# A state space computed in blocks of four tokens with a Toeplitz part on TensorE, in a two-layer fp32 decoder trunk

## The reference

```
for l in range(2):
    h = rmsnorm(x, norm_mix[l])
    u, sq, sk, sv, dq, dk, dv, gate_logits = split(h @ w_in[l])
    y_ssm = gelu(s5_ssm(u, ...))                # 32 groups of 16 channels, 64 complex states each
    glu_a, glu_b = split(y_ssm @ ssm_w_glu[l]); y_ssm = glu_a * sigmoid(glu_b)
    y_sb = stick_breaking_attention(sq, sk, sv)
    y_da = rmsnorm(differential_attention(rope(dq), rope(dk), dv, lam)) * (1 - lam_init)
    x = x + sum(sigmoid(gates) * (branches @ w_branch[l])) @ w_out[l]
    m = rmsnorm(mem, norm_mem[l])               # 256 memory tokens, the same in both layers
    x = x + cross_attention(rmsnorm(x, norm_cross[l]) @ w_xq[l], m @ w_xkv[l]) @ w_xo[l]
    x = x + square(relu(rmsnorm(x, norm_mlp[l]) @ w_up[l])) @ w_down[l]
return rmsnorm(x, norm_final)

# s5_ssm, for each group: lam_bar = exp(lam * dt), b_bar = ((lam_bar - 1) / lam) * b
#   s[t] = lam_bar * s[t-1] + b_bar @ u[t];   y[t] = Re(c @ s[t]) + d * u[t]
```

## Time and profile before

| | us |
|---|---|
| median of three runs | 1209.06 (1208.31 to 1209.67) |
| the profiled execution, its own time | 1207.81 |
| its span | 1206.1 |
| TensorE busy in the span | 1090.8 (90%) |
| VectorE busy | 876.0 (73%) |
| ScalarE busy | 565.9 (47%) |
| GpSimd busy | 302.8 (25%) |

### The profile page before, as it was taken

How to read it: one execution, slowest core, us unless ns; L and a number is a source line. 1 busy time by engine, 2 the same in 40 slices (tenths; PEclk the granted TensorE clock), 3 DMA queues, 4 the chain that set the end, 5 groups by cost and what they waited for, 6 DMA issues and landing times. The chain is left out here.

```text
span 1206.1 us, 18306 instructions
## 1 busy us (share of the span) xinstructions
PE 1090.8 (90%) x6855; PEld 963.5 (80%) x6855; DVE 876.0 (73%) x1236; ACT 565.9 (47%) x874; POOL 302.8 (25%) x362
## 2 busy tenths in 40 slices
PE   3997898879999799999979798988899987999996
PEld 3985677769989688998869566767699976998995
DVE  5769999986877475555567899999778756555553
ACT  4643433236565454444444443332475654544442
POOL 0496775510000000000008868653100000000000
PEclk7997988889999989999979988987899998999998
DMA  7652323323554445565646422422255543555550
GB/s 254 184 156 68 109 71 105 100 76 132 184 182 145 128 136 185 187 191 192 186 117 180 122 70 71 124 86 78 98 175 181 177 131 99 183 191 190 184 186 35
DMA packets 138076, 170.34 MB, mean 141 GB/s; under 512 B 18043, under 2 KB 96005, under 8 KB 137989
## 3 DMA queue, kind: packets, MB, share of 16 engines
q1 hardware_dynamic: 137572, 168.91, 44.3%
q10 hardware_dynamic: 416, 0.26, 0.1%
HBM read 168.11 MB, written 1.05 MB: 140 GB/s over the span
## 5 line engine op out<-in xcount | busy, mean ns | idle before, releaser
L1124 DVE TENSOR_TENSOR s_w_lo<-s_raw,s_w_hi 128x1024 fp32r<-128x1024 f32 x312 | 419.5, 1369 | 165.5 <-ACT s_w_hi L742 161.0
L742 ACT ACTIVATE s_w_hi<-s_raw 128x1024 fp32r<-128x1024 f32 x312 | 320.9, 1054 | 186.7 <-PE p_T L1586 114.6
L1584 PE MATMUL p_T<-s_hT_hi,s_w_hi 128*128 128x256 f32 x1152 | 341.9, 297 | 14.2 <-DVE s_hT_lo L1184 14.2
L1585 PE MATMUL p_T<-s_hT_lo,s_w_hi 128*128 128x256 f32 x1152 | 336.8, 292 | 0.0
L1586 PE MATMUL p_T<-s_hT_hi,s_w_lo 128*128 128x256 f32 x1152 | 336.4, 292 | 0.0
L1584 PEld LDWEIGHTS p_T<-s_hT_hi,s_w_hi 128*128 128x128 f32 x1152 | 233.0, 202 | 26.5 <-issue 26.0
L1585 PEld LDWEIGHTS p_T<-s_hT_lo,s_w_hi 128*128 128x128 f32 x1152 | 233.2, 202 | 0.5
L1586 PEld LDWEIGHTS p_T<-s_hT_hi,s_w_lo 128*128 128x128 f32 x1152 | 232.1, 201 | 0.0
L1584 PE MATMUL p_A<-s_w_hi,s_bT_hi 128*128 128x512 f32 x320 | 124.9, 390 | 2.4 <-DVE s_bT_lo L1124 2.4
L1585 PE MATMUL p_A<-s_w_lo,s_bT_hi 128*128 128x512 f32 x320 | 124.7, 390 | 0.0
L1586 PE MATMUL p_A<-s_w_hi,s_bT_lo 128*128 128x512 f32 x320 | 124.5, 389 | 0.0
(11 more groups left out here) (249 smaller groups left out, 1824.4 us busy)
## 6 DMA issues: line engine op xcount, KB each, us to landing
s_raw<-in_w_in SPq DMA_DIRECT2D x104, 512.0 KB, 3.6
s_raw<-in_w_up SPq DMA_DIRECT2D x64, 512.0 KB, 3.7
s_raw<-in_w_down SPq DMA_DIRECT2D x64, 512.0 KB, 3.6
s_raw<-in_w_branch SPq DMA_DIRECT2D x24, 512.0 KB, 3.6
s_raw<-in_w_out SPq DMA_DIRECT2D x16, 512.0 KB, 3.6
s_raw<-in_w_xkv SPq DMA_DIRECT2D x16, 512.0 KB, 3.5
s_raw<-in_ssm_w_glu SPq DMA_DIRECT2D x8, 512.0 KB, 3.5
s_raw<-in_w_xq SPq DMA_DIRECT2D x8, 512.0 KB, 3.5
```

The costliest lines, as they stand in the source:

```text
L742: return nc.scalar.activation(o, i, f, **kw)
L1124: return V.tensor_tensor(o, i0, i1, op)
L1584: mm(o, lhi, rhi, start=first, stop=False, **kw)
L1585: mm(o, lhi, rlo, start=False, stop=False, **kw)
```

## The change

The state space works on blocks of BL = 4 tokens, NB = 64 blocks. State is carried from block to block only: `ssm_in(kb)` (4 of them, 4 tiles each) multiplies u, laid out by blocks in `uB`, by tables `bt` that hold four powers of the decay; VectorE turns, scans 64 blocks with decay to the fourth, and turns back. What happens inside a block is a 4x4 block-Toeplitz matrix `kt` per tile on TensorE, added with `ct` in `ssm_out(kb)`.

These tables (`ct`, `kt`, `bt`, the phase table, the decay `dect`) must be made per layer. Stages `p_spread`, `p_params`, `p_angle`, `p_cos`, `p_ct`, `p_cv`, `p_b0`, `p_bv`, `p_k`, `p_bt` do it on all engines, and `tables` and `zero_b` on POOL. For layer 0 they lie behind units 0 to 6, for layer 1 behind units 50 to 70 of layer 0 (its MLP). The new state space then runs behind units 7 to 12 in layer 0 and 2 to 7 in layer 1. The evacuation of u becomes 32 small copies into `uB` (16 on VectorE, 16 on ScalarE). The memory tokens are read anew in each layer into `att` and transposed behind units 33 and 34; their row statistics are made once, in layer 0, and scale xk and xv. `raw` has 6 slots and `w_hi` 4, so AHEAD falls to 2. The parameters of layer 1 are loaded in layer 0's MLP, ahead of chunk 97 on SP's queue.

```diff
-SSM_STEPS = STILES // 2
+BL = 4
+NB = T // BL
+TAB_STEPS = 6
...
-LO, HI = 10, 6
+LO, HI = 6, 4
 AHEAD = HI // 2
...
+    def pre(tgt, u):
+
+        after(u["angle"], "p_angle", tgt)
+        after(u["cos"], "p_cos", tgt)
+        after(u["ct"], "p_ct", tgt)
+        for r in range(2):
+            after(u["cv"][r], "p_cv", tgt, r)
+        after(u["b0"], "p_b0", tgt)
+        for r in range(2):
+            after(u["bv"][r], "p_bv", tgt, r)
+        for n in range(4):
+            after(u["k"][n // 2], "p_k", tgt, n)
+        for n in range(8):
+            after(u["bt"][n // 2], "p_bt", tgt, n)
+
+    if l == 0:
+        pre(0, dict(angle=0, cos=0, ct=1, cv=(1, 2), b0=3, bv=(3, 4), k=(4, 4), bt=(4, 5, 5, 6)))
+        first = 7
+        pre(1, dict(angle=up0 + 6, cos=up0 + 7, ct=up0 + 9, cv=(up0 + 11, up0 + 13), b0=up0 + 15,
+                    bv=(up0 + 16, up0 + 18), k=(up0 + 18, up0 + 20),
+                    bt=(up0 + 21, up0 + 22, up0 + 23, up0 + 24)))
+        after(up0 + 4, "p_spread", 1)
+        after(up0 + 5, "p_params", 1)
+        for u in (up0 + 4, up0 + 5):
+            side[u].sort(key=lambda s: s[0] != "p_spread")
+    else:
+        first = 2
+    for kb in range(4):
+        after(first + kb, "ssm_in", kb)
+        after(first + 1 + kb, "ssm_out", kb)
+    after(first + 5, "gelu")
...
-    for i in range(SSM_STEPS):
-        after(7 + 2 * i, "ssm_in", i)
-        after(8 + 2 * i, "ssm_rot", i)
-        after(min(10 + 2 * i, 23), "ssm_out", i)
-    after(23, "gelu")
...
-    after(33, "memg")
+    after(33, "mem_turn", 0)
+    after(33, "mem_turn", 1)
+    after(34, "mem_turn", 2)
+    after(34, "mem_turn", 3)
+    if l == 0:
+        after(33, "stats", "mem", 0)
+        after(33, "stats", "mem", 1)
+        after(35, "norm", "mem")
...
+                    if c == 1 and l == 0:
+                        load_params(0)
+                    if c == 2 * AT_UNIT["up", 1, 0] and l + 1 < DEPTH:
+                        sp.wait_ge(*st.at(prm_read, 1))
+                        sp.wait_ge(*st.at(h_ready, 3 * KD // 2))
+                        load_params(1)
+                    if c == 2 * AT_UNIT["branch", 1, 1]:
+                        sp.wait_ge(*st.at(da_hi, NT))
+                        load(mem_raw, a["mem"][0].rearrange("(t p) d -> p t d", p=P), mem_landed)
...
+                pool.wait_ge(*st.at(*freed(l, "X1", ("p_ct", t))))
+                nc.gpsimd.tensor_copy(dect[:, :, :], DEC4.unsqueeze(2).broadcast_to([P, STILES, NB])).then_inc(*st.mid())
+                pool.wait_ge(*st.mine())
+                nc.gpsimd.memset(dect[:, :, 0:1], 0.0).then_inc(*st.sig(dect_ready, t + 1))
+
+            def zero_b(st, t, l):
+
+                pool.wait_ge(*st.at(h_ready, KD // 2 if l == t else 3 * KD // 2))
+                for h in range(2):
+                    rows, o = slice(STATES * h, STATES * h + STATES), GC * (1 - h)
+                    pool.wait_ge(*st.mine())
+                    nc.gpsimd.memset(bN0[rows, :, :, o:o + GC], 0.0).then_inc(*st.mid())
+                    for r in range(2):
+                        ins = nc.gpsimd.memset(bN[rows, r, :, :, o:o + GC], 0.0)
+                        ins.then_inc(*st.sig(b_zeroed, t + 1)) if h and r else ins.then_inc(*st.mid())
 
...
+                if l == 0:
+                    tables(st, 0, 0)
+                    zero_b(st, 0, 0)
+                for w in range(2):
+                    if st.last:
+                        pool.wait_ge(*st.mine())
+                    rotate(w)
+                if l + 1 < DEPTH:
+                    pool.wait_ge(*st.mine())
+                    tables(st, l + 1, l)
+                    zero_b(st, l + 1, l)
                 pool.wait_ge(*st.mine())
...
+                def p_b0(t):
+
+                    dve.wait_ge(*st.at(mat_landed, 6 * (t + 1)))
+                    dve.wait_ge(*st.at(pow_ready, t + 1))
+                    dve.wait_ge(*st.at(b_zeroed, t + 1))
+                    for r in range(2):
+                        times_b(t, r, 4, 1, lambda rows, c: bN0[rows, r, :, c:c + GC].unsqueeze(1)).then_inc(*st.mid())
+                        dve.wait_ge(*st.mine())
+                    n = 2 * GC
+                    tt(diag_d, ident[0:n, 0:n].unsqueeze(1).broadcast_to([n, STILES, n]),
+                       col[0:n, R_D:R_D + STILES].unsqueeze(2).broadcast_to([n, STILES, n])).then_inc(*st.sig(b0_ready))
...
+                    tt(v[:, :, :, 1:NB], io, turned(0)).then_inc(*st.mid())
+                    tt(t0[:, :, :, 1:NB], io, turned(1)).then_inc(*st.sig(*freed(l, b, s)))
...
+                    for r in range(2):
+                        vf = v[:, r, :, :].rearrange("p i m -> p (i m)")
+                        V.tensor_tensor_scan(vf, dect[:, sl, :].rearrange("p i m -> p (i m)"), vf, 0.0, ALU.mult, ALU.add)\
+                         .then_inc(*st.mid())
...
+                                mm(bank[b][:, c:c + NB], ct[:, r, i, :], st_y[:, r, i * NB:i * NB + NB],
+                                   start=(r == 0), stop=False)
+                            ins = mm(bank[b][:, c:c + NB], kt[:, i, :], uB[:, i, :], start=False, stop=True)
+                        ins.then_inc(*st.sig(y_done))
```

More of the change, by code:

```diff
@@ L196, in side_stages @@
     after(AT_UNIT["xo", 1], "norm", "mlp")
-    return side
-SIDE = side_stages()
+    for u in range(7, 27):
+        side[u].sort(key=lambda s: RANK.get(s[0], 7))
+    return side
+RANK = {"da_o": -1, "da_t": 1, "sb_p": 0, "da_p": 0, "sb_u": 1, "sb_s": 2, "da_s": 2, "da_c": 3, "da_n": 3,
+        "ssm_in": 4, "ssm_out": 6}
+SIDES = [side_stages(l) for l in range(DEPTH)]
 ACT_PREP_EARLY = set(range(0, 16)) | set(range(AT_UNIT["up", 0, 0], NU))
@@ L268, in stage_banks @@
         [["A0", "A1", "A3", "A2"][s[1]]] if s[0] == "xa_p" else [])
+NORMS = ["mix", "cross", "mlp"]
+NORM_SEQ = [(l, n) for l in range(DEPTH) for n in ("mix", "mem", "cross", "mlp") if n != "mem" or l == 0]
 KEYS = [None] * NU
@@ L424, in hybrid_trunk @@
         lo_made = signal("w_lo_made", NC)
-        lo_made_pool = signal("w_lo_made_pool", sum(2 * (pool_cols(u) > 0) for u in range(NU)))
         chunk_done = signal("chunk_done", NC)
[L427 to L433, removed]
+        prm_landed = counted("prm_landed", 9 * DEPTH, step=16)
@@ L491, in wslot @@
             return tile.rearrange("p (k n) -> p k n", k=UNITS[u][2] // 2)
-        def pooled(u):
-            return sum(2 * (pool_cols(i) > 0) for i in range(u + 1))
         def f32(ap):
@@ new lines, in p_k @@
+                def p_k(s):
+                    t, n = s[1:]
+                    b = stage_banks(s)[0]
+                    act.wait_ge(*st.at(*full_at(l, b, s)))
+                    src = bank[b][:, :].rearrange("p (i c) -> p i c", c=P)
+                    for j in range(BL):
+                        rows = slice(32 * j, 32 * j + 32)
+                        ins = fn(kt[rows, 4 * n:4 * n + 4, 32 * j:P], src[0:32, :, 0:P - 32 * j])
+                        ins.then_inc(*st.sig(*freed(l, b, s))) if j == BL - 1 else ins.then_inc(*st.mid())
@@ new lines, in p_angle, with places, spread, parts @@
+                    reduce_angle(st, TH, KK, THR)
+                    V.tensor_scalar(THR, THR, PI_SAFE, -PI_SAFE, ALU.min, ALU.max).then_inc(*st.sig(angle_ready))
+                def places(m, p):
+                    return m.unsqueeze(3).broadcast_to([P, p, STILES, GC])
+                def spread(m, p):
+                    return m.unsqueeze(1).broadcast_to([P, p, STILES, GC])
+                def parts(t, p):
+                    o = att[:, 0:2048] if t == 0 else qk[:, :, :].rearrange("p k n -> p (k n)")
+                    return [o[:, 1024 * i:1024 * i + p * STILES * GC].rearrange("p (n i c) -> p n i c", n=p, c=GC)
+                            for i in range(2)]
@@ new lines, in p_cv @@
+                def p_cv(t, r):
+                    if r == 0:
+                        dve.wait_ge(*st.at(*freed(l, "X1", ("p_ct", t))))
+                        dve.wait_ge(*st.at(pow_ready, t + 1))
+                    q = parts(t, 3)
+                    tt(q[0], spread(c_raw[:, r, :, :], 3), places(POWERS[:, 0, :, :], 3)).then_inc(*st.mid())
+                    tt(q[1], spread(c_raw[:, 1 - r, :, :], 3), places(POWERS[:, 1, :, :], 3)).then_inc(*st.mid())
+                    dve.wait_ge(*st.mine())
+                    for h in range(2):
+                        rows = slice(STATES * h, STATES * h + STATES)
+                        o = ct[rows, r, :, :].rearrange("p i (n h c) -> p n i h c", n=BL, h=2)[:, 1:BL, :, h, :]
+                        ins = tt(o, q[0][rows], q[1][rows], ALU.subtract if r else ALU.add)
+                        ins.then_inc(*st.sig(ct_ready)) if h else ins.then_inc(*st.mid())
@@ new lines, in times_b @@
+                def times_b(t, r, i, n, out):
+                    q = parts(t, n)
+                    tt(q[0], spread(b_raw[:, r, :, :], n), places(FACTORS[:, 0, i:i + n, :], n)).then_inc(*st.mid())
```

(8 more changed lines are left out.)

1040 lines of the change are left out of this document (525 added, 515 removed).

## The result

The changed kernel takes 1280.36 us (median of four runs, 1277.34 to 1283.25) against 1208.68 for the kernel before on the same chip: the ratio is 1.0594, 95% interval 1.0561 to 1.0627. The forecast had slower, by 4, and a range to 1238; it is slower by 72. Its profiled execution took 1278.16 us, with a span of 1276.4, 70.3 more than before.

The account below looks back on a forecast made before the run. It took TensorE to bound the MLP, and TensorE and VectorE, both nearly full and handing work to each other, the mixed parts. Terms -50 - 51 + 52 + 11 + 6 + 36 = +4 gave 1213 us, range 1183 to 1238.

Parts of the forecast that it names:

- the short products on TensorE: Mixed parts: 160 instructions of 63 or 64 columns at 0.06 to 0.08 us each, 10 to 13 us in layer 0.
- the gelu's block: Mixed part, layer 0: the new gelu of 32 small activations, counted within 8 us of stalls from attention chains.
- the lead of two units: Around cross attention: two units of lead in place of three start units behind the norms 2 to 3 us late.
- the small loads: Layer 0's MLP: 15 parameter loads on SP's queue ahead of chunk 97 cost +2 us.
- Mixed part, layer 0, -50: Units 7 to 27: VectorE relieved, TensorE's clock up, about 170 us against 220.3; bounds -38 and -58.
- Mixed part, layer 1, -51: Same work with the state space behind units 2 to 7: 262.8 to about 212 us; bounds -40 and -60.
- Start, +52: Layer 0 to unit 7's end: TensorE runs dry waiting for tables and zeroed b; 128 to 133 us instead of 79.
- Cross attention, +11 and +6: Branches and cross attention, layers 0 and 1: memory-token transposes, statistics in layer 0 and shorter lead add 11 and 6 us.
- MLP, +36: Layer 0's MLP making layer 1's tables: TensorE products +14, wait for the chain +20, parameter loads +2 us.
- Rival A: Tables cheap enough: GpSimd's chain little held up, MLP chain under 51 us, no stall there, start +44; 1185 us, chance 0.33.
- Rival B: Mixed parts gain less: attention chains set the pace, clock stays 0.88 and 0.90, saving 38 and 40; 1236 us, chance 0.16.
- Rival C: GpSimd fully locked out by VectorE, MLP chain taking 89 us: +18, 1231 us, chance 0.11.

Follow-up runs that it names:

- e_double: Changed kernel with each of ssm_in's 64-instruction products issued twice, 128 more short instructions in the two layers: 1287.64 us.
- e_zero: Changed kernel with the six memsets of b ahead of the table chain on GpSimd instead of behind it, in both layers: 1232.99 us.
- e_klate: Changed kernel with memsets first, loads between chunks, y copied in four stages, earlier preparations around cross attention, plus layer 0's p_k and p_bt later: 1189.31 us.
- e_best: As e_klate, with layer 0's memory-token statistics in two halves behind units 33 and 34 instead of both behind 33: 1187.82 us.
- e_ring: Kernel before with only the rings shortened, 6 slots of raw and 4 of hi in place of 10 and 6: 1228.3 us.
- e_params: Changed kernel with layer 1's 15 small loads issued two by two between the MLP's chunks instead of all ahead of chunk 97: 1269.75 us.

## Why the prediction was wrong

The sign was right and the size wrong, by 67 us. The sign proves little: the sum was +4, and the forecast gave slower 0.54. Four terms were sized wrong: the short products on TensorE, the gelu's block, the lead of two units, and the small loads. By its own steps:

1. *Mixed part, layer 0, -50.* Came -33.5. The VectorE half of the step held: 109.8 us, low halves at 1221 ns. The TensorE half failed twice. The "160 instructions with 63 or 64 columns", put at "10 to 13 us", were mis-sized: 24.0 us busy, and 18.7 at the 0.117 each of e_double. The row used was of a 128-column product, taken as if the time went with the columns. And the 8 us of stalls, "(the new gelu of 32 small activations too)", took the gelu as work and not as a block: it cost 10.2 us here. The two, some 6.7 (18.7 against 12) and 10.2, come to about the 16.5 us that are missing. (A slip of the working besides: at full clock with no gap 179 x 0.88 is 157.5, a bound of -63 and not -58.)
2. *Mixed part, layer 1, -51.* Came -25.7, from the same two: 12.9 us are the block. Here the state space stands behind units 2 to 7 where little lies beside it, which the forecast took as equal to layer 0. With the block gone the part still takes 224.2 us against 212 forecast, TensorE being busy 216.3 of them. The short products are some 7 of these 12 us by the price above. The other 5 are open; the unit at a clock of 0.71 that e_double made 4.7 us shorter is of that size.
3. *Start, +52.* Came +57.6. The mechanism was right: TensorE's hole lasted from 64.3 to 96.3 us (65 to 98 forecast), the last memset ended at 92.0 (91 to 97 forecast) and VectorE waited 27.0 us for it. GpSimd's chain began at 41 and not 45, and took 51 us. Two pieces behind the hole were some 5 us too small each: `p_k` took 14.6 us and not 10, and from there to the end of unit 7 it was 25.7 and not 21. The first multiplication came 7.2 us earlier (21.1 against 28.3), 5 forecast. e_zero shows that 19 to 20 us of the start hung on the order of the memsets. Another part was `p_k` on TensorE in front of unit 5: with it behind units 5 and 6, unit 7 ends at 110.4 (e_klate) and 108.2 (e_best) instead of 117.2. Of the 29 us that are left against 79.0, TensorE is busy for 15.9 (76.5 us in 108.2, against 60.6 in 79.0) and idle for 13.3; this was not taken apart further.
4. *Cross attention, +11 and +6.* Came +15.8 and +8.6. The two-unit lead was put at 2 to 3 us a layer, and e_ring measured 10 in the kernel before. This term is wrong by a factor of three to five.
5. *MLP, +36.* Came +47.5. The wait was forecast at 20 and was 22.0, the table products at 14 and were 16.6; the loads were put at 2 us and were worth 7.3 in this part (e_params). That the wait came so close is partly luck: the chain took 65 us and not 70, but VectorE came to the wait 43 us after the chain's start (527.3 to 570.4) and not 51, and the two errors cancel.

Rival A fell: the chain took from 527.3 to 592.3, 65 us, and not under 51. Rival B had the right place and a wrong reason, since the clock did rise (0.96 and 0.94). Rival C asked for 89 us and is refuted in that form: GpSimd lost time to VectorE (34 products of 128x16 took 15.49 us there and 9.54 in the start), but the chain took 65.

## What to carry to other kernels

Price a block by its longest uninterrupted stretch on an in-order engine, against the lead of the work behind it: 13 us in one piece stopped TensorE for 9 to 12 us whichever engine did the copies, and with the copies in four pieces and the gelu later both stops were gone. Price a short product from a product as short; where none is in the trace, don't halve a longer one: here 63 columns cost 0.117 us and 128 columns 0.13. And before a shared lead is shortened to make room, run the old kernel with the short lead: that single run would have shown a cost of 20 us, where 4 to 6 were put down.

## What was not expected of the hardware

A fp32 product instruction with 63 columns costs TensorE 0.117 us (e_double); eight transposes of 128 columns took 1.03, 0.13 each, so half the columns saved next to nothing. The pieces of y, 32 partitions by 128 elements from PSUM, took 0.41 us each on either engine (12.32 us for 30 on ScalarE, 13.10 for 32 on VectorE). The pieces of u have the same shape and took 0.29 each on ScalarE (4.66 us for 16); they are written without gaps and y's to every fourth element, but which of their differences makes the 0.12 us no run here shows. A wait of 2.3 us on TensorE was followed by a unit at a clock of 0.71, and added work which closed the wait to 0.5 us made that unit shorter. And behind the same hole of 32 us, with the same program, the clock came back after 7 us in one run and after more than 19 in another.
